# Convolved feed-forwards computed in groups of four output tiles by 26 block products, with the weight sums on GpSimd

## What is computed

```
D_FF = ((8 * D_MODEL // 3) + 127) // 128 * 128     # 2816 = 22 tiles of 128
h    = rms_norm_2(x, gain)
up   = h @ w_up                                    # 1024 -> 2 * 2816
up   = causal depthwise convolution of width 3 along the tokens, plus bias
y    = (gelu(first half of up) * second half of up) @ w_down
```

## Time and profile before

| what | value |
|---|---|
| timed runs | 3982.04, 3983.37 (median), 3984.84 us |
| profiled execution | 3973.42 us, span 3971.6 us |
| PE busy | 3854.7 us, 97% of the span |
| DVE, ACT, POOL busy | 2344.7, 914.7, 1639.9 us |
| granted TensorE clock, mean | 0.99 |

### The profile page before, as it was taken

How to read it: one execution, slowest core, us unless ns; L and a number is a source line. 1 busy time by engine, 2 the same in 40 slices (tenths; PEclk the granted TensorE clock), 3 DMA queues, 4 the chain that set the end, 5 groups by cost and what they waited for, 6 DMA issues and landing times. The chain is left out here.

```text
span 3971.6 us, 58645 instructions
## 1 busy us (share of the span) xinstructions
PE 3854.7 (97%) x21473; PEld 3136.5 (79%) x21473; DVE 2344.7 (59%) x4349; ACT 914.7 (23%) x2022; POOL 1639.9 (41%) x1485
## 2 busy tenths in 40 slices
PE   7998999999999999999899999999999999999999
PEld 4886868887885688866688688888666787788888
DVE  3776579524553665235559576883364486757861
ACT  3433222103333221014501211111143201111111
POOL 2335257533320465421156463454311374714543
PEclk9999999999998999999999999999999999999999
DMA  7222254335432333362133232332623233223332
GB/s 263 72 55 89 85 155 135 97 91 160 133 96 70 106 85 98 87 130 54 33 91 90 75 85 67 93 85 86 120 52 67 54 88 84 78 62 95 84 85 85
DMA packets 626830, 369.31 MB, mean 93 GB/s; under 512 B 71306, under 2 KB 594987, under 8 KB 625364
## 3 DMA queue, kind: packets, MB, share of 16 engines
q1 hardware_dynamic: 613112, 346.13, 32.2%
q10 hardware_dynamic: 13532, 20.69, 1.7%
HBM read 348.40 MB, written 11.01 MB: 90 GB/s over the span
## 5 line engine op out<-in xcount | busy, mean ns | idle before, releaser
L738 POOL TENSOR_TENSOR weight_slot<-weight_slot 128x512 f32<-128x512 f32 (+1 forms) x76 | 109.3, 1438 | 483.7 <-DMA weight_slot<-in_ffn_w_up 261.5
L832 PE MATMUL psum<-h_normed,weight_slot 128*128 128x256 f32 x1280 | 289.6, 379 | 0.0
L4145 PE MATMUL psum<-sums_of_h,weight_slot 128*128 128x256 f32 x1280 | 282.8, 379 | 0.0
L4145 PEld LDWEIGHTS psum<-sums_of_h,weight_slot 128*128 128x128 f32 x1280 | 243.2, 190 | 33.1
L832 PEld LDWEIGHTS psum<-h_normed,weight_slot 128*128 128x128 f32 x1280 | 243.2, 190 | 33.1
L4362 DVE SCALAR_TENSOR_TENSOR o_conv<-padded,vectors,o_conv 128x512 f32<-128x512 f32 x240 | 226.6, 1014 | 0.0
L832 PE MATMUL psum<-sums_of_h,weight_slot 128*128 128x256 f32 x960 | 220.5, 379 | 3.7 <-POOL weight_slot L744 3.7
L4145 PE MATMUL psum<-h_normed,weight_slot 128*128 128x256 f32 x960 | 217.6, 383 | 5.2 <-PEq L209 5.2
L4145 PEld LDWEIGHTS psum<-h_normed,weight_slot 128*128 128x128 f32 x960 | 184.6, 192 | 31.4 <-issue 5.7
L832 PEld LDWEIGHTS psum<-sums_of_h,weight_slot 128*128 128x128 f32 x960 | 182.2, 190 | 29.2 <-POOL weight_slot L744 4.5
L5238 DVE SCALAR_TENSOR_TENSOR u<-raw,vectors,u 128x511 f32<-128x511 f32 (+1 forms) x160 | 163.5, 1042 | 60.1 <-ACT u L5210 48.4
(11 more groups left out here) (719 smaller groups left out, 9183.8 us busy)
## 6 DMA issues: line engine op xcount, KB each, us to landing
weight_slot<-in_w_ffn_in SPq DMA_DIRECT2D x88, 512.0 KB, 6.4
weight_slot<-in_ffn_w_up SPq DMA_DIRECT2D x88, 512.0 KB
weight_slot<-in_w_gate SPq DMA_DIRECT2D x64, 512.0 KB
weight_slot<-in_w_in SPq DMA_DIRECT2D x40, 512.0 KB, 5.3
weight_slot<-in_dsw_w_in SPq DMA_DIRECT2D x36, 512.0 KB, 6.4
weight_slot<-in_gdn_w_in SPq DMA_DIRECT2D x32, 512.0 KB, 5.4
tile_ahead<-in_w_ada SPq DMA_DIRECT2D x16, 1024.0 KB, 5.2
weight_slot<-in_w_branch SPq DMA_DIRECT2D x64, 256.0 KB, 3.3
```

Of the source, the lines that this page charges most:

```text
L738: nc.gpsimd.tensor_tensor(b(self.S1), b(self.A21), b(self.A22), ALU.add).then_inc(self.folded, 1)
L832: last = nc.tensor.matmul(c.ps[:, 4 * bank + r // 2, (r % 2) * self.HALF:(r % 2 + 1) * self.HALF], self.slot(s)[:, b * 512 + k * P:b * 512 ...
L4145: last = nc.tensor.matmul(c.ps[:, 4 * s + r // 2, (r % 2) * self.HALF:(r % 2 + 1) * self.HALF], c.slots[s][:, b * 512 + k * P:b * 512 + (k ...
```

## The change

`conv_ffn` now builds a `GroupProducts` as `swiglu` does, with these differences. All 28 weight sums of a group run on GpSimd. The four sums of gated tiles run on DVE (`sum_group`). ScalarE's gelu (`bend`) is moved into the next group's `snapshots`, and DVE's multiplication with it. The room for the combinations of input tiles is the `shared` buffer; `c.x` is copied to HBM once `late.ready` says that it is final.

```diff
+    def sum_group(self, engine, unit, i, more):
...
+        engine.wait_ge(self.multiplied, i * 4 + (2 * more + 2 + self.before))
+        unit.tensor_tensor(t1, b12, b11, ALU.subtract).then_inc(self.t_hidden, 1)
+        engine.wait_ge(self.t_hidden, i * 8 + (4 * more + 1))
+        unit.tensor_tensor(t2, b22, t1, ALU.subtract).then_inc(self.t_hidden, 1)
+        unit.tensor_tensor(b12, b22, b12, ALU.subtract).then_inc(self.t_hidden, 1)
+        engine.wait_ge(self.t_hidden, i * 8 + (4 * more + 2))
+        unit.tensor_tensor(t4, b21, t2, ALU.subtract).then_inc(self.t_hidden, 1)
...
         keep(self.C_EARLY, self.C)
+        if between[0] is not None:
+            between[0]()
...
         keep(self.D_SUMS, self.D)
+        if between[1] is not None:
+            between[1]()
...
-            ffn = SevenProducts(c, sems[0:10], hidden, sums_in, sums_hidden, work)
-            ffn.before = 2
+            ffn = GroupProducts(c, sems[0:10], sems[48:56], hidden, sums_hidden, extra,
+                                room[:, :, :].rearrange("p (a k) n -> p a k n", k=2), snaps)
+            ffn.before, ffn.work = 2, extra[:, 8:11, :]
+            ffn.whole_freed = convolved
...
             def _(sp):
+                sp.wait_ge(late.ready, KT)
                 ffn.sync(sp, lambda n0, g: layer_columns(w_up, layer, n0 + g * F2, P),
...
                 late.gpsimd(pool)
-                ffn.gpsimd(pool, whole=True)
+                pool.sem_inc(ffn.folded, 4 * FT)
+                pool.sem_inc(ffn.late_mixed, ffn.LATE)
+                with pool.Fori(0, ffn.GROUPS // 2) as i:
+                    for s in range(2):
+                        ffn.fold_group(pool, i, s)
+                        ffn.fold_late(pool, nc.gpsimd, i, s)
+                ffn.gpsimd_out(pool)
                 add.gpsimd(pool)
...
-                ffn.tensor(pe, late.ready, whole=True)
+                with pe.Fori(0, ffn.GROUPS // 2) as i:
+                    for s in range(2):
+                        pe.wait_ge(ffn.loaded[s], ffn.landed_group(i))
+                        ffn.multiply_group(pe, i, s)
+                pe.wait_ge(ffn.gathered, ffn.SUMS * ffn.GROUPS + 17)
+                ffn.tensor_out(pe)
...
+                with act.Fori(0, ffn.GROUPS // 2) as i:
                     for s in range(2):
+                        at, back = tile_of(i, s), tile_of(i, s - 1)
+                        ffn.snapshots(act, i, s, (lambda: bend(back, 0), lambda: bend(back, 1)))
+                        act.wait_ge(ffn.gathered, i * (2 * ffn.SUMS) + ((s + 1) * ffn.SUMS + 17))
+                        filter_tile(at, 0, grouped)
+                        act.wait_ge(ffn.gathered, i * (2 * ffn.SUMS) + (s + 2) * ffn.SUMS)
+                        filter_tile(at, 1, grouped)
...
-                ffn.sum_inputs_early(dve, late.ready)
+                ffn.sum_x(dve, late.ready, 80 + 16 * layer)
...
+                with dve.Fori(0, ffn.GROUPS // 2) as i:
                     for s in range(2):
-                        ffn.combine_in(dve, i, s, raw[:, s, 0, :], raw[:, s, 1, :])
-                        convolve(i, s, lambda s, t: raw[:, s, t, :])
-                    ffn.sum_hidden(dve, i)
+                        for t in range(2):
+                            multiply(tile_of(i, s - 1), t)
+                        ffn.sum_group(dve, nc.vector, i, s)
+                        ffn.gather(dve, i, s, raw[:, 0, 0, :], raw[:, 0, 1, :], raw[:, 1, 0, :], raw[:, 1, 1, :])
+                        for t in range(2):
+                            convolve(tile_of(i, s), t, grouped)
```

More of the change, by code:

```diff
@@ L965 @@
     GROUPS = FT // 2 - 1
+    whole_freed = None
     B_EARLY, D_SUMS, A_EARLY, C_EARLY, A_NEXT, B_NEXT = range(6)
@@ L1066, in fold_group @@
         put(w(3, 2), X(2), w(3, 2))
+    def sum_group(self, engine, unit, i, more):
+        near, far = self.hidden[:, ds(i * 2 + more, 1), :], self.hidden[:, ds(i * 2 + (more + self.KH), 1), :]
+        b11, b12 = near[:, :, 0:self.HALF], near[:, :, self.HALF:S]
+        b21, b22 = far[:, :, 0:self.HALF], far[:, :, self.HALF:S]
+        t1, t2, t4 = (self.sums_hidden[:, j, ds(i * 2 + more, 1), :] for j in range(3))
+        engine.wait_ge(self.multiplied, i * 4 + (2 * more + 2 + self.before))
+        unit.tensor_tensor(t1, b12, b11, ALU.subtract).then_inc(self.t_hidden, 1)
+        engine.wait_ge(self.t_hidden, i * 8 + (4 * more + 1))
+        unit.tensor_tensor(t2, b22, t1, ALU.subtract).then_inc(self.t_hidden, 1)
+        unit.tensor_tensor(b12, b22, b12, ALU.subtract).then_inc(self.t_hidden, 1)
+        engine.wait_ge(self.t_hidden, i * 8 + (4 * more + 2))
+        unit.tensor_tensor(t4, b21, t2, ALU.subtract).then_inc(self.t_hidden, 1)
     def fold_late(self, engine, unit, i, s):
@@ L5218, in _ @@
                     act.wait_ge(ffn.done, 2 + s + 1)
-                    filter_tile(0, s, whole)
-                with act.Fori(1, FT // 2) as i:
+                    filter_tile(first_tile, s, whole)
+                with act.Fori(0, ffn.GROUPS // 2) as i:
                     for s in range(2):
-                        act.wait_ge(ffn.combined, i * 8 + (4 * s + 12))
-                        filter_tile(i, s, lambda s, t: raw[:, s, t, :])
+                        at, back = tile_of(i, s), tile_of(i, s - 1)
[4 more added lines that the diff above has]
+                        filter_tile(at, 1, grouped)
+                for s in range(2):
+                    bend(tile_of(ffn.GROUPS // 2 - 1, 1), s)
+                act.wait_ge(ffn.done, FT + 2)
+                act.dma_start(c.x[:, :, :], c.kept).then_inc(ffn.x_back, 16)
                 add.scalar(act)
@@ L5235, in convolve @@
+                def convolve(at, s, of):
                     for t in range(2):
[L5236 to L5243, removed]
-                                ins.then_inc(convolved, 1)
@@ L5254, in _ @@
[L5254 to L5262 removed]
+                        dve.wait_ge(filtered, at(4, 2 * s + t + 1))
@@ new lines, in multiply @@
+                def multiply(at, s):
+                    dve.wait_ge(gelued, at(2, s + 1))
+                    dve.wait_ge(convolved, at(4, 2 * s + 2))
+                    nc.vector.tensor_tensor(hidden[:, ds(at(1, s * ffn.KH), 1), :], u[:, s, 0, :], u[:, s, 1, :], ALU.mult
+                                            ).then_inc(ffn.multiplied, 1)
+                for s in range(2):
+                    convolve(first_tile, s, whole)
+                ffn.sum_x_late(dve)
+                with dve.Fori(0, ffn.GROUPS // 2) as i:
+                    for s in range(2):
+                        for t in range(2):
[4 more added lines that the diff above has]
+                            convolve(tile_of(i, s), t, grouped)
@@ L5263, in _ @@
+                for t in range(2):
+                    multiply(tile_of(ffn.GROUPS // 2 - 1, 1), t)
+                ffn.sum_hidden(dve, nc.vector, ffn.GROUPS)
+                dve.wait_ge(ffn.gathered, ffn.SUMS * (ffn.GROUPS + 1))
+                dve.sem_inc(ffn.combined, 4)
+                dve.wait_ge(ffn.x_back, 16)
                 add.vector(dve)
```

89 lines of the change are left out of this document (47 added, 42 removed).

## The result

The changed kernel takes 4026.5 us (median of 4, 4024.3 to 4028.9), the kernel before 3984.1 (3982.0 to 3989.7). The ratio is 1.0104, 95% interval 1.0089 to 1.0119: 42.4 us slower. The forecast was 4026.

The account below looks back on a forecast made before the run. PE bounds the kernel before; POOL, slowed by VectorE, would bound the loop at 26.0 us a group. That adds 21.4 us a layer, 43 in all: 3973.4 becomes 4016, plus 9.95 for timed runs, 4026 us; range 4000 to 4054.

Parts of the forecast that it names:

- PE's rows: Up-projection loop: a group is 104 rows on PE, 22.4 us, where a round before was 112 rows, 24.2 us.
- POOL's group: Up-projection loop: 28 sums, 19.7 us alone, 25.7 with VectorE's surcharge, taken as 26.0 for imperfect meshing.
- 0.43 for 512 columns: Surcharge in us on a POOL sum from each 512-wide VectorE instruction with two SBUF operands, ten a group.
- 0.17 for 256: Surcharge in us on a POOL sum from each 256-wide VectorE instruction, ten a group in sum_group and gather.
- 0.32: Alternative surcharge in us for each 512-wide instruction, read from wider POOL sums; it makes POOL's group 24.6 us.
- As full as POOL: VectorE's group in the loop: 24.7 us of work, 25.2 to 25.7 with its waits for PE.
- The rival at 27.5 us: VectorE bounds the loop at 27.5 us a group, with 2.8 us of waits: 4053 us, chance 11%.
- The port held whole: Rival: VectorE and POOL block each other for full instruction lengths, 31.3 us a group, 4121 us, chance 3%.
- Where PE waits: PE stands at round 10 of each group for late sum 7, 3.6 us each time.
- The start: Before the loop: first weights land after 2 MB of residual, at 2443.8 in place of 2440.39.
- The end: After the last group PE waits about 0.5 us for gather; the down projection starts at 2706.4, against 2684.99.
- The clock: Sign: PE's granted clock stays at the 2.4 GHz level; if pauses lower it, groups get longer.

Follow-up runs that it names:

- experiment 5: Changed kernel with a group's eight convolution instructions reading an unused PSUM bank and ScalarE's first copy and second gelu moved earlier: 3969.0 us, 0.9962.
- 7: Changed kernel with two of a group's four joined tiles written to PSUM banks 4 and 5, computing all of the reference: 3986.2 us, 1.0011.
- experiment 2: Changed kernel with two more VectorE copies of 128x256 from PSUM in each convolution group: 4026.1 us, 1.0109.
- Experiment 3: Changed kernel with four of a group's eight late GpSimd sums done on 8 columns in place of 256: 4002.3 us, 1.0048.

## Why the prediction was right

The cause was right and so was the sum. That it came out to 0.5 us is luck: some of its parts were off and offset each other. Where a time of after is set against one of the forecast, 6.15 us are taken off, the shift at VectorE's first input sum (2433.58 - 2427.43).

- **PE's rows.** 104 rows in 22.4 us: shown by experiment 5.
- **POOL's group.** Sum 25.7, taken 26.0, measured 25.8. The 0.3 for two engines that mesh badly wasn't there. 0.43 for 512 columns and 0.17 for 256 are borne out by experiments 5 (at least 0.42) and 7 (their sum); 0.32 would have given 24.6.
- **VectorE.** "As full as POOL" was a little too much: it is busy for 161.8 of the 180 us from 2480 on, 23.2 a group where the sum had 24.7 and the signs asked for 24, and experiment 2 shows room for 0.8 us a group. In this group it stands still for 2.7 us before PE's round 11. The rival at 27.5 us falls. Experiment 3 shows what would have come next, the ring through VectorE and ScalarE at 24.4 to 24.9. ScalarE was said not to be in the way; that held only because POOL was slower, and the sum of its 9 us had left out 2.6 us of ACT_TABLE_LOAD in every second group.
- **The port held whole.** 31.3 us a group falls, and with it that each instruction blocks the other for its full length: 1.13 us a pair, not 1.45. The Trainium skill (SBUF — State Buffer, Who interferes with whom) calls the shared port pair an exclusive lock, says of VectorE's 2-port modes that it is held for the whole instruction, and of a VectorE instruction with two SBUF inputs that it contends with a GpSimd instruction that reads SBUF. The prediction had carried the whole length over to the last of these. Whom it hits agrees here: each row of the convolution with a PSUM operand stays at 0.74 to 0.75. No run tells a port that is shared throughout from one that a sum holds for only a part of its 0.70 us (by estimate 1.13 - 0.75 = 0.38).
- **Where PE waits.** At round 10 for late sum 7, in every group, as forecast, but in the first layer for 0.85 to 2.45 us, 1.8 on the mean, and not 3.6. The rest is in short waits at earlier rounds (0.66 at 2542.42, for a sum of L1032; 1.15 at 2613.20, for ScalarE's first copy) and in slower rows.
- **The start.** POOL at 2449.40 - 6.15 = 2443.25, forecast 2443.8. Late sum 7 of the first group releases PE at 2464.7, forecast 2465.0.
- **The end.** PE waits for `gather` for 2.70 us, not 0.5. I had given the 0.5 without a row. In the last group VectorE begins to gather only at 2702.96 and then goes through it in 9.9 us without a wait (9.65 in the sum): it is behind PE there, and not waiting for it. This +2.2 and the nine groups at -0.23 cancel, which nothing in the working provided for: the down projection is at 2706.5, forecast 2706.4.
- **The clock.** After the wait of 2.44 us that ends at 2497.00 the pairs of rows stand 0.85 us apart (2498.01, 2498.86) in place of 0.43, at a mean granted clock of 0.69 from 2495 to 2500, which takes in the 1.2 GHz level; in the next five it is 0.97. The sign that the clock would stay at the 2.4 GHz level failed. In the 180 us from 2480 on the mean is 0.97, by estimate 0.03 x 25.8 = 0.8 us a group. PE is busy for 164.7 of them, 23.6 a group or 1.2 over its 22.4, of which the rest goes with the ends of the waits, where single rows are longer (0.70 at 2470.88 against 0.59). It lies in time in which PE would wait for POOL: PE still waits at round 10 of each group, and the groups are POOL's 25.8.

## What to carry to other kernels

When sums move to GpSimd, count beside them how many of VectorE's instructions have two operands in SBUF, and add their surcharge to GpSimd and VectorE alike, before comparing with PE; one operand in a free PSUM bank buys it back, here 40 us for two banks. Then look past the bound: a group that is spread over four in-order engines has a second one right behind it, and here it was the queue of a ScalarE that is busy for a little over a third of the loop (groups 24.3 in place of 22.4), by its order and the ACT_TABLE_LOAD rows in it together. Look for both in the trace before pricing an engine by its work alone. To find out which it is, add work to one engine at a time: the bound answered in full (+29 us), and the engine that was merely busy not at all, for work that fitted into its waits.

## What the runs showed of the hardware that I had not expected

- A GpSimd sum of 8 columns takes 0.16 to 0.61 us from start to start in the loop, where one of 256 takes 0.70 alone. The mean of the four is 0.47, so a sum with a 32nd of the columns still costs two thirds of a whole one.
- The two instructions of the convolution don't share alike in the pairs: the starts are 1.36 and 0.90 us apart by turns (2585.05, 2586.41, 2587.31), the rows 1210 and 987 ns long. Only over both is the step steady, 2.26 us for two sums of GpSimd, so a surcharge should be read from starts over a whole turn and not from one row.
- Writing a joined tile to PSUM costs VectorE hardly more than to SBUF: 692 ns for 512 columns against 677 to 687.
